# One slot and one tick: moving the side work of a three-block transformer kernel in TensorE's order

## The chip, the cores and the metric

The kernel runs on one core of a Trainium2 chip. The metric is device time in microseconds, the median of three runs. TensorE, VectorE, ScalarE, GpSimd and SyncE each work through their own list of instructions in order; semaphores tie the lists together.

## The reference, cut to what matters

256 tokens of width 2048 pass through three transformer blocks. Only the first one is touched:

```
h    = rms_norm(x)
p_r, p_k, p_v, z_r, q, k, v, z_a, m_r, m_a = split(h @ w_in)
y_r  = rwkv7(h, p_r, p_k, p_v) * silu(z_r)           # a recurrence over the tokens, 16 heads of 64
y_a  = chunk_band_attention(q, k, v) * silu(z_a)     # 16 heads of 64
x    = x + rms_norm((sigmoid(m_r) * (y_r @ w_r) + sigmoid(m_a) * (y_a @ w_a)) @ w_out)
```

The attention is softmax(q k + bias) v over a band of chunks. The recurrence is

```
S = S * w_t + (S @ -kk_t) (kk_t * a_t) + v_t k_t ;  y_t = S r_t
```

with kk normalised per head and y normalised per head afterwards (mean, variance, reciprocal root). The kernel computes it in chunks of 64 tokens.

## The kernel before

**Main work.** All large products are a stream of slots: 512 rows of a weight matrix by 256 columns, in fp32 made of a high and a low half. Per slot TensorE does 8 products of 512 columns (high half, L2516) and 8 of 256 columns (low half, L2520). ScalarE makes the high half of the weights (L2419), VectorE the low half (L2426), both two slots ahead ("the split of slot q+2"); SyncE loads the weights. Four slots make a block in the sections of this document. The sections stand at these slots: qkv from 0, za from 48, rkv from 64, gates from 112, zr from 176, branch from 192. At a block's end ScalarE copies a part of the sums out of PSUM (L2027), VectorE adds the rest (L2129), and the block is rescaled by the norm: by VectorE in rkv and zr (L2133), by GpSimd in gates (L2071). In rkv VectorE then mixes neighbouring tokens (L2139, L2142). These follow the split on VectorE.

**Side work.** The attention, the recurrence and other small work run as threads beside the stream. A thread is a set of generators, one per engine, that yield ticks. A tick t stands at start + t x pace, in slots, and class Beside runs it at the next of the three places of a slot on that engine: q, q+0.34 and q+0.67. On TensorE the place q stands ahead of the slot's products, q+0.34 after four wide ones, q+0.67 after eight (in rkv every second slot has the narrow products first). On VectorE the place q stands after L2129 of a block that just ended and ahead of the split of slot q+2 and of the rescaling; q+0.34 stands after both. On ScalarE q stands after L2027 and ahead of the split. So the ticks alone set each engine's order of instructions.

**Attention1** (two threads, for even and odd pairs of heads, always called one behind the other) has four rounds of 12 ticks at a pace of 0.85. Steps of a round: VectorE scales q (L767), ScalarE reverses k and v into place (L797, L798), TensorE turns v and makes the scores of the first head of the pair (L824 to L832), VectorE adds the bias and takes the maximum (L773 to L777), TensorE makes the second head's scores, which needs the first ones read ("scored0", L774), then exp on ScalarE (L805, L807), probabilities on VectorE (L781 to L784), their transposes (L842) and the products with v (L848 to L850) on TensorE, and the gate on VectorE (L789).

**Rwkv** (two threads, even and odd pairs of heads) starts one slot into gates, at slot 113, at a pace of 0.28. Its first norms are done ahead of the rounds: squares on VectorE (L953, L955), sums on TensorE (`norms`), a reciprocal root in Newton steps on VectorE (`roots`, L959, L90 to L95, L965), spread on TensorE (`norm_spread`), product (`normed`, L969). Then four rounds of 66 ticks begin at tick FIRST = 8: decay logits (TensorE), tanh (ScalarE), "sigmoid" (VectorE, L987), cumulated sums (TensorE), exponentials (ScalarE, L1072 to L1075), r_hat, z_hat, b_hat, k_hat (VectorE, L994 to L999), products ab and ak (TensorE), a triangular inverse in five doubling steps (y1/xx1 to y5/xx5; copies L1086 on ScalarE, sums L1016 and L1018 on VectorE), four chunk steps (w, sa, st for c = 0 to 3; L1090 on ScalarE, L1023, L1035, L1037 on VectorE), then mean, variance (L1045, L90 to L95), its spread and the normalised y (L1052 to L1057). All products of this class stand at L1105. The next round's norms are done within a round.

zr's blocks on VectorE (L2174) need y of the rounds; branch needs all of it.

Of the kernel before, what the change touches and what calls it, by code (L numbers as in the profile page):

```python
# [118 lines left out]
def build_kernel(nc, I, out_dram):  # L119
    ctx = ExitStack()  # L120
    with ctx:
# [171 lines left out]
        def par(name, c=0, n=1):  # L293
            return prm[:, rows[name] + c:rows[name] + c + n]
# [569 lines left out]
        class Rwkv:  # L864
# [11 lines left out]
                PE += [f"w{c}", f"sa{c}"] + ([f"st{c}"] if c < 3 else [])  # L876
            PE += ["o", "mean", "var", "var_spread"]
            TICKS = 66
            FIRST = 8

            def __init__(self, th, take, more):
                self.th = th
# [31 lines left out]
            def gpsimd(self, pool):  # L914
                dv, ac, pe_, po = self.dv, self.ac, self.pe_, self.po
                for i in range(4):
                    j, t0 = 2 * i + self.th, self.FIRST + self.TICKS * i
                    yield t0
# [24 lines left out]
            def vector(self, v):  # L943
# [5 lines left out]
                def squares(i):  # L949
                    k = k_[:, 2 * i + self.th, :]  # L950
                    if i:
                        dv.wait(v, "b_hat", i - 1)
                    self.dk.did(v.tensor_scalar(self.kn, k, par("k_k", 2 * i + self.th), None, ALU.mult), "kk")  # L953
                    self.dk.wait(v, "kk", i)
                    self.dk.did(v.tensor_tensor(self.sqr, self.kn, self.kn, ALU.mult), "kk_squared")  # L955

                def roots(i):
                    self.pk.wait(v, "kk_norm", i)
                    self.dk.did(v.tensor_scalar(self.nrm, x[:, 128:132], 1e-30, None, ALU.max), "norm_copied")  # L959
                    if self.th == 1:  # L960
                        for rw in rwkv:
                            rw.dk.wait(v, "norm_copied", i)
                        norm_roots.did(rwkv_root.run(v, *rwkv_eight), "rooted")
                        norm_roots.wait(v, "rooted", i)
                        norm_roots.did(v.tensor_scalar(rwkv_eight[1], rwkv_eight[1], 1e12, None, ALU.min), "inverted")  # L965

                def normed(i):
                    self.pk.wait(v, "norm_spread", i)
                    self.dk.did(v.tensor_tensor(self.kn, x[:, 256:512], self.kn, ALU.mult), "kk_normed")  # L969
                    self.dk.wait(v, "kk_normed", i)  # L970
                for i in range(4):
                    j, t0 = 2 * i + self.th, self.FIRST + self.TICKS * i
                    pr = lambda name: par(name, j)
                    if i == 0:
                        yield 0
                        v.wait_ge(mixed, 36)
                        v.wait_ge(masks_made, MASKS)
                        v.wait_ge(lora_activated, 9)
                        squares(0)
                        yield 2  # L980
                        roots(0)
                        yield 6
                        normed(0)
                    yield t0 + 2
                    ac.wait(v, "decay", i)
# [60 lines left out]
                    if self.th == 1:  # L1046
                        for rw in rwkv:
                            rw.dv.wait(v, "variance", i)
                        deviation_roots.did(rwkv_root.run(v, *rwkv_eight), "inverted")
                    yield t0 + 66  # L1050
                    pe_.wait(v, "var_spread", i)
                    dv.did(v.tensor_tensor(self.y, y[:, 0:256], self.y, ALU.mult), "y_normed")  # L1052
                    dv.wait(v, "y_normed", i)
# [6 lines left out]
            def scalar(self, act):  # L1060
# [3 lines left out]
                for i in range(4):  # L1064
                    t0 = self.FIRST + self.TICKS * i
                    yield t0 + 1
# [31 lines left out]
            def tensor(self, pe):  # L1098
# [13 lines left out]
                def norms(i):  # L1112
                    self.dk.wait(pe, "kk_squared", i)
                    for t in range(2):
                        m = mm(x[:, 128 + 2 * t:130 + 2 * t], self.sqr[:, t * P:(t + 1) * P], headpair)
                    self.pk.did(m, "kk_norm")

                def norm_spread(i):
                    norm_roots.wait(pe, "inverted", i)
                    self.pk.did(spread(x[:, 256:512]), "norm_spread")  # L1120
                for i in range(4):
                    j, t0 = 2 * i + self.th, self.FIRST + self.TICKS * i
                    if i == 0:
                        yield 1
                        norms(0)
                        yield 4
                        norm_spread(0)
                    yield t0
                    if i:
# [110 lines left out]
                    for t in range(2):  # L1240
                        m = mm(x[:, 256 + 2 * t:258 + 2 * t], self.ysq[:, t * P:(t + 1) * P], headpair)
                    pe_.did(m, "var")
                    yield t0 + 65
                    deviation_roots.wait(pe, "inverted", i)
                    pe_.did(spread(y), "var_spread")

# [959 lines left out]
        at = lambda name, b=0.0: S[name].slot0 + b * S[name].slots  # L2206
# [2 lines left out]
        threads.append(Thread("lora", 0, 0.5, sync=lora_sync, gpsimd=lora_pool, vector=lora_vector, tensor=lora_tensor, scalar=lora_scalar))  # L2209
        att1 = [Attention1(0, low, 7424, variance), Attention1(1, high, 14336, variance_t)]  # L2210
        for th in range(2):
            att1[th].thread(at("rkv", 0.25), 0.85)
        pieces = [[(high, 2048, 6656)], [(high, 6656, 8192), (low, 7424, 9472), (high, 14336, 16384)]]

        def taker(spans):
# [383 lines left out]
```

## Time and profile before

| | |
|---|---|
| median of 3 runs | 3461.02 us (3460.91 to 3462.06) |
| the profiled execution's own time | 3464.4 us |
| its span, first to last instruction | 3462.7 us |
| mean granted TensorE clock | 0.989 |
| TensorE busy | 3373.7 us, 97% |
| VectorE busy | 2204.5 us, 64% |
| ScalarE busy | 1540.7 us, 44% |
| GpSimd busy | 295.4 us, 9% |

Stages of the profile: the side work of Attention1 lies between about 225 and 335 us (rkv), that of Rwkv between 393 and 820 us (gates and zr). A row of a timeline gives start, duration, engine, line, operation, output and inputs; in brackets stands the idle time of the engine just before it and what ended it. A granted clock of 1.00 is TensorE's full speed (2.4 GHz), 0.50 the lower level (1.2 GHz).

### The profile page before, as it was taken

To read this page: it belongs to the slowest core of one execution; us is meant where nothing else is said; L and a number is where in the kernel's file an instruction comes from. 1 tells how busy PE (TensorE), PEld (TensorE's weight loads), DVE (VectorE), ACT (ScalarE), POOL (GpSimd) and SP (SyncE) were. 2 spreads that over 40 slices of the span, in tenths; PEclk is the share of its full clock that TensorE was granted. 3 is DMA by queue.
4 is the path that set the end of the run, shared out by engine and by line. 5 is a ranking of instruction groups with operands and counts; after the bars stand their busy time and mean duration, and the time that the engine had idled before them with its cause. 6 is when DMAs were issued, how large, how long until landed. Compare 5 with 4: busy or idle time off the path is not lost.

```text
span 3462.7 us, 52014 instructions
## 1 busy us (share of the span) xinstructions
PE 3373.7 (97%) x21718; PEld 2915.4 (84%) x21718; DVE 2204.5 (64%) x3044; ACT 1540.7 (44%) x2117; POOL 295.4 (9%) x318
## 2 busy tenths in 40 slices
PE   8999999999989999999999999999999999999998
PEld 7888877778878888888888888888888888888887
DVE  5567655556667576777666446655677866446654
ACT  4454433334553445544544444444354544334443
POOL 3100122220011101110100000001000100000000
PEclk9999999999999999999999999999999999999999
DMA  5554433335635555655555665565554556556554
GB/s 190 178 180 154 137 111 111 111 107 184 195 126 160 185 158 167 197 161 170 194 182 185 195 193 186 184 200 180 175 158 159 183 179 211 194 182 194 190 199 146
DMA packets 550751, 592.98 MB, mean 171 GB/s; under 512 B 16757, under 2 KB 511733, under 8 KB 550262
## 3 DMA queue, kind: packets, MB, share of 16 engines
q1 hardware_dynamic: 550518, 589.66, 52.6%
q8 instruction: 172, 2.82, 0.3%
q14 instruction: 61, 0.50, 0.0%
HBM read 583.24 MB, written 6.32 MB: 170 GB/s over the span
## 4 chain that ended last, share of the span: by engine, by line
PE 88%; DVE 7%; ACT 2%; issue 2%; DMA 1%; POOL 0%; SPq 0%; DVEq 0%; ACTq 0%; POOLq 0%
PE gp L2516 45%; PE gp L2520 24%; PE gp L2501 7%; PE sidep L1105 4%; PE gp L2506 3%; DVE w_parts L2426 2%; ACT w_parts L2419 1%; DMA high<-bias_rows 0%; DVE stage L2133 0%; ACT lo_half L2027 0%; PE sidep L560 0%; PE sidep L1345 0%; DVE stage L2129 0%; DVE low L2165 0%; PE sidep L1430 0%
## 5 line engine op out<-in xcount | busy, mean ns | idle before, releaser
L2426 DVE TENSOR_TENSOR w_parts<-ring,w_parts 128x1024 fp32r<-128x1024 f32 x1084 | 1365.8, 1282 | 456.1 <-ACT w_parts L2419 454.9
L2516 PE MATMUL gp<-x_parts,w_parts 128*128 128x512 f32 x5840 | 1482.9, 398 | 11.4 <-issue 5.5
L2419 ACT ACTIVATE w_parts<-ring 128x1024 fp32r<-128x1024 f32 x1084 | 1109.0, 1052 | 453.5 <-PE gp L2506 189.0
L2516 PEld LDWEIGHTS gp<-x_parts,w_parts 128*128 128x128 f32 x5840 | 1062.9, 190 | 215.9 <-issue 10.3
L2520 PEld LDWEIGHTS gp<-x_parts,w_parts 128*128 128x128 f32 x5840 | 773.3, 192 | 47.9 <-issue 5.9
L2520 PE MATMUL gp<-x_parts,w_parts 128*128 128x256 f32 x5840 | 802.3, 285 | 2.6 <-DVE w_parts L2426 2.6
L2027 ACT ACTIVATE lo_half<-gp 128x512 f32<-128x512 f32 x239 | 142.8, 597 | 896.5 <-PE gp L2516 460.9
L2516 PE MATMUL gp<-ff_parts,w_parts 128*128 128x512 f32 x1792 | 430.8, 391 | 0.0
L2516 PEld LDWEIGHTS gp<-ff_parts,w_parts 128*128 128x128 f32 x1792 | 328.6, 188 | 63.0
L2129 DVE TENSOR_TENSOR stage<-gp,lo_half 128x512 f32<-128x512 f32 x168 | 116.0, 690 | 378.7 <-ACT lo_half L2027 377.8
L2501 PE MATMUL gp<-w_parts,ff_parts 128*128 128x512 f32 x1024 | 273.7, 389 | 0.0
L2520 PEld LDWEIGHTS gp<-ff_parts,w_parts 128*128 128x128 f32 x1792 | 230.9, 191 | 10.6 <-issue 0.9
L2520 PE MATMUL gp<-ff_parts,w_parts 128*128 128x256 f32 x1792 | 235.4, 283 | 0.3 <-DVE w_parts L2426 0.3
L2501 PEld LDWEIGHTS gp<-w_parts,ff_parts 128*128 128x128 f32 x1024 | 192.3, 188 | 39.8
L528 POOL TENSOR_TENSOR low<-low 128x512 f32<-128x512 f32 (+1 forms) x38 | 58.9, 1557 | 1238.2 <-ACT low L519 648.9
L2506 PE MATMUL gp<-w_parts,ff_parts 128*128 128x512 f32 x512 | 157.7, 389 | 0.0
L2129 DVE TENSOR_TENSOR high<-gp,lo_half 128x512 f32<-128x512 f32 x63 | 43.5, 690 | 166.4 <-ACT lo_half L2027 166.3
L2043 ACT ACTIVATE ff_parts<-stage 128x512 fp32r<-128x512 f32 x64 | 40.5, 632 | 166.6 <-DVE stage L2167 166.6
L2506 PEld LDWEIGHTS gp<-w_parts,ff_parts 128*128 128x128 f32 x512 | 96.1, 188 | 20.0
L1105 PEld LDWEIGHTS sidep<-high 64*64 64x64 f32 x1696 | 62.6, 136 | 42.9 <-issue 18.6
L2071 POOL TENSOR_TENSOR high<-high,rstd 128x512 f32<-128x512 f32 x40 | 58.7, 1467 | 459.8 <-DVE high L2129 459.8
L1105 PE MATMUL sidep<-high 64*64 64x64 f32 (+1 forms) x1696 | 75.9, 237 | 16.2 <-DVE high L997 4.6
(391 smaller groups left out, 1868.6 us busy)
## 6 DMA issues: line engine op xcount, KB each, us to landing
ring<-w_in SPq DMA_DIRECT2D x220, 1024.0 KB, 5.1
ring<-w_ff SPq DMA_DIRECT2D x128, 1024.0 KB, 5.6
ring<-w_up SPq DMA_DIRECT2D x64, 1024.0 KB, 5.8
ring<-w_down SPq DMA_DIRECT2D x64, 1024.0 KB, 5.0
ring<-w_out SPq DMA_DIRECT2D x48, 1024.0 KB, 5.2
ring<-w_branch_attn SPq DMA_DIRECT2D x8, 1024.0 KB, 5.2
ring<-w_branch_rwkv SPq DMA_DIRECT2D x8, 1024.0 KB, 5.2
gate_scratch<-stage SPq DMA_DIRECT2D x16, 256.0 KB, 2.3
```

The source lines that it names most:

```text
L528: m = pool.tensor_tensor(self.acc[k], self.acc[k], self.sq[b - 1][k], ALU.add)
L1105: return pe.matmul(out, lhs, rhs, start=start, stop=stop, skip_group_check=True)
L2027: act.activation(lo_half[:, k % 2], gp[:, k % 2, :, 1, :], ACT.Copy).then_inc(lo_copied, 1)
L2043: act.activation(ff_parts[:, 2 * b:2 * b + 2, 0, :], st, ACT.Copy).then_inc(ff_high_split, 1)
L2071: pool.tensor_tensor(to, to, over(rstd, 2), ALU.mult).then_inc(scaled_by_pool, 1)
L2129: v.tensor_tensor(to, gp[:, k % 2, :, 0, :], lo_half[:, k % 2], ALU.add).then_inc(block_evacuated, 1)
L2419: act.activation(w_parts[:, q % PARTS, 0], ring[:, u % RING, SLOT * (q % 2):SLOT * (q % 2) + SLOT, :], ACT.Copy).then_inc(high_split, 1)
L2426: v.tensor_tensor(w_parts[:, q % PARTS, 1], ring[:, u % RING, SLOT * (q % 2):SLOT * (q % 2) + SLOT, :], w_parts[:, q % PARTS, 0].bitcast(F ...
L2501: pe.matmul(wide_sums(k, t), operand(s, b, s.chunks * n + c)[:, half, tokens], w[:, 0, c, :], start=(n == 0 and c == 0 and half == 0), sto ...
L2506: m = pe.matmul(wide_sums(k, t), operand(s, b, s.chunks * n + c)[:, 0, tokens], w[:, 1, c, :], start=False, stop=(n == s.slots - 1 and c = ...
L2516: return pe.matmul(gp[:, k % 2, j, :, :], w_parts[:, q % PARTS, 0, c, j * P:(j + 1) * P], operand(s, b, SLOT * n + c), start=(n == 0 and c ...
L2520: return pe.matmul(gp[:, k % 2, j, 0, :], w_parts[:, q % PARTS, 1, c, j * P:(j + 1) * P], operand(s, b, SLOT * n + c)[:, 0, :], start=Fals ...
```

## The change

Five numbers and two conditions in the ticks:

- FIRST goes from 8 to 9: all rounds of the recurrence a tick (0.28 slots) later, on all four engines.
- Its first norms: TensorE's sums go from tick 1 to 4, its spread from 4 to 7; VectorE's root from 2 to 4.8, the product from 6 to 8. The squares stay at tick 0.
- The last round's spread of the variance on TensorE goes from tick 65 of the round to 67, the normalised y on VectorE from 66 to 68; in the other rounds they stay.
- Attention1 starts at slot 66, not 65: all its steps one slot later, on all engines and SyncE.

Nothing is added or taken away.

```
-            FIRST = 8
+            FIRST = 9
...
                         squares(0)
-                        yield 2
+                        yield 4.8
                         roots(0)
-                        yield 6
+                        yield 8
                         normed(0)
...
-                    yield t0 + 66
+                    yield t0 + (66 if i < 3 else 68)
                     pe_.wait(v, "var_spread", i)
...
-                        yield 1
+                        yield 4
                         norms(0)
-                        yield 4
+                        yield 7
                         norm_spread(0)
...
-                    yield t0 + 65
+                    yield t0 + (65 if i < 3 else 67)
                     deviation_roots.wait(pe, "inverted", i)
...
-            att1[th].thread(at("rkv", 0.25), 0.85)
+            att1[th].thread(at("rkv", 0.5), 0.85)
```

**VectorE at the end of block 88 (in rkv), third round of Attention1.** L773 to L777 read the scores; L2129 begins what follows the block's end, L2142 ends it. Before:

```order
L773 TENSOR_TENSOR low<-sidep,low 128x128
L774 TENSOR_TENSOR low<-sidep,low 128x256
...
L2129 TENSOR_TENSOR stage<-gp,lo_half 128x2x256
L2426 TENSOR_TENSOR w_parts<-ring,w_parts 128x1024
L2133 TENSOR_TENSOR stage<-stage,rstd 128x2x256
L2139 TENSOR_TENSOR high<-stage 128x512
L2142 SCALAR_TENSOR_TENSOR high<-high,prm,stage 128x256 x2
```

The change:

```order
L2129 TENSOR_TENSOR stage<-gp,lo_half 128x2x256
L2426 TENSOR_TENSOR w_parts<-ring,w_parts 128x1024
L2133 TENSOR_TENSOR stage<-stage,rstd 128x2x256
L2139 TENSOR_TENSOR high<-stage 128x512
L2142 SCALAR_TENSOR_TENSOR high<-high,prm,stage 128x256 x2
L773 TENSOR_TENSOR low<-sidep,low 128x128
L774 TENSOR_TENSOR low<-sidep,low 128x256
```

The first scores of the round stood ahead of the block's end and now stand behind its mixing.

**TensorE from slot 87 on, the same round.** L824 to L832 with x2 of ident are v's transposes and the first scores; the L831 and L832 without them are the second scores. Before:

```order
L832 MATMUL sidep<-high 128x256
L2516 MATMUL gp<-x_parts,w_parts 128x512 x4
L2520 MATMUL gp<-x_parts,w_parts 128x256 x16
L2516 MATMUL gp<-x_parts,w_parts 128x512 x8
L831 MATMUL sidep<-low,high 128x128
```

The change:

```order
L832 MATMUL sidep<-high 128x256
L2516 MATMUL gp<-x_parts,w_parts 128x512 x12
L2520 MATMUL gp<-x_parts,w_parts 128x256 x8
L831 MATMUL sidep<-low,high 128x128
```

The second scores stood at the end of block 88 and now stand one slot behind it, at slot 89.

**TensorE at slots 113 to 115, the first norms of Rwkv.** headones,high is the sum of squares, ident,smalls the spread of the root, sidep<-low the decay logits. Before:

```order
L2516 MATMUL gp<-x_parts,w_parts 128x512 x4
L1105 MATMUL sidep<-headones,high 128x2 x4
L2516 MATMUL gp<-x_parts,w_parts 128x512 x4
L2520 MATMUL gp<-x_parts,w_parts 128x256 x8
L2516 MATMUL gp<-x_parts,w_parts 128x512 x4
L1105 MATMUL sidep<-ident,smalls 64x128 x8
L2516 MATMUL gp<-x_parts,w_parts 128x512 x4
L2520 MATMUL gp<-x_parts,w_parts 128x256 x8
L2516 MATMUL gp<-x_parts,w_parts 128x512 x4
L1105 MATMUL sidep<-low 128x128 x4
```

The change:

```order
L2516 MATMUL gp<-x_parts,w_parts 128x512 x8
L2520 MATMUL gp<-x_parts,w_parts 128x256 x8
L2516 MATMUL gp<-x_parts,w_parts 128x512 x4
L1105 MATMUL sidep<-headones,high 128x2 x4
L2516 MATMUL gp<-x_parts,w_parts 128x512 x4
L2520 MATMUL gp<-x_parts,w_parts 128x256 x8
L1105 MATMUL sidep<-ident,smalls 64x128 x8
L2516 MATMUL gp<-x_parts,w_parts 128x512 x8
L1105 MATMUL sidep<-low 128x128 x4
```

The sums of squares come a slot later, the spread two thirds of a slot, the decay logits a third.

**ScalarE at the end of block 172 (in gates), head of the fourth round of Rwkv.** L1068 is tanh for "sigmoid", L2027 the block's copy, L2419 a pass of high halves, L1072 to L1075 the exponentials of one pair of heads. Before:

```order
L1068 ACTIVATE low<-sidep 128x256
L2419 ACTIVATE w_parts<-ring 128x1024
L2027 ACTIVATE lo_half<-gp 128x512
L1072 ACTIVATE high<-sidep,consts 128x256
...
L1075 ACTIVATE smalls<-sidep 128x4
L2419 ACTIVATE w_parts<-ring 128x1024 x2
```

The change:

```order
L1068 ACTIVATE low<-sidep 128x256
L2027 ACTIVATE lo_half<-gp 128x512
L2419 ACTIVATE w_parts<-ring 128x1024
L1072 ACTIVATE high<-sidep,consts 128x256
...
L1075 ACTIVATE smalls<-sidep 128x4
L2419 ACTIVATE w_parts<-ring 128x1024
```

The exponentials stood ahead of both passes behind the block's end and now stand between them; tanh moved the other way, behind the pass ahead of the block's end.

At the end of the last round the variance on TensorE comes a third of a slot later and its spread a whole slot (190, not 189); VectorE's order is the same there.

## Rows read from the trace of the kernel before

**Rows 1.** The page, part 1: busy time, share of the span, instructions.

```profile
PE 3373.7 (97%) x21718; PEld 2915.4 (84%) x21718; DVE 2204.5 (64%) x3044; ACT 1540.7 (44%) x2117; POOL 295.4 (9%) x318
```

**Rows 2.** The page, part 4: the chain that ended last, by engine.

```profile
PE 88%; DVE 7%; ACT 2%; issue 2%; DMA 1%; POOL 0%; SPq 0%; DVEq 0%; ACTq 0%; POOLq 0%
```

**Rows 3.** TensorE's waits, 340 to 840 us: total us, times, longest us.

```profile
PE sidep L1105 <- DVE high L987: 5.5, 4, 1.6
PE sidep L1105 <- DVE high L997: 4.6, 2, 3.4
...
PE sidep L1105 <- DVE high L955: 3.4, 2, 2.5
PE sidep L1105 <- DVE smalls L95: 2.4, 1, 2.4
...
PE gp L2520 <- DVE w_parts L2426: 0.4, 1, 0.4
```

**Rows 4.** TensorE's waits, 25 to 340 us, the one in Attention1.

```profile
PE sidep L842 <- DVE low L784: 1.3, 2, 1.1
```

**Rows 5.** Windows, TensorE: length, busy (instructions), granted clock, DMA share, GB/s.

```profile
401.20:404.60 3.40, 3.40 (x14) 0.51 0.43 132
725.50:729.00 3.50, 3.50 (x40) 0.51 0.14 45
814.30:817.70 3.40, 3.08 (x19) 0.50 0.08 12
```

**Rows 6.** Timeline, TensorE, ab and ak of the fourth round.

```profile
724.55 5.38 PE L1105 MATMUL sidep<-high 64*64 64x128 f32 x64 [3.42 <-DVE high L997]
```

**Rows 7.** Timeline, TensorE, the last round's spread of the variance.

```profile
814.62 1.97 PE L1105 MATMUL sidep<-ident,smalls 128*64 128x128 f32 x16 [2.36 <-DVE smalls L95]
```

**Rows 8.** Timeline, TensorE, two slots without side work.

```profile
378.13 2.08 PE L2520 MATMUL gp<-x_parts,w_parts 128*128 128x256 f32 x16
...
383.69 2.08 PE L2520 MATMUL gp<-x_parts,w_parts 128*128 128x256 f32 x16
```

**Rows 9.** Timeline, VectorE, behind the end of block 88.

```profile
310.59 0.69 DVE L2129 TENSOR_TENSOR stage<-gp,lo_half 128x512 f32<-128x512 f32 x1 [1.85 <-ACT lo_half L2027]
311.54 1.23 DVE L2426 TENSOR_TENSOR w_parts<-ring,w_parts 128x1024 fp32r<-128x1024 f32 x1 [0.25 <-ACT w_parts L2419]
...
314.13 0.88 DVE L2142 SCALAR_TENSOR_TENSOR high<-high,prm,stage 128x256 f32<-128x256 f32 x2
314.93 0.28 DVE L773 TENSOR_TENSOR low<-sidep,low 128x128 f32<-128x128 f32 x1
...
316.10 0.28 DVE L773 TENSOR_TENSOR high<-sidep,high 128x128 f32<-128x128 f32 x1
```

**Rows 10.** Timeline, TensorE, first row behind the end of block 88.

```profile
309.86 0.49 PE L831 MATMUL sidep<-low,high 64*128 64x128 f32 x2
```

**Rows 11.** Timeline, ScalarE, k and v of one pair staged.

```profile
301.72 0.42 ACT L797 ACTIVATE low<-high 128x256 f32<-128x256 f32 x1 [4.59 <-DVE high L767]
302.04 0.40 ACT L798 ACTIVATE low<-high 128x256 f32<-128x256 f32 x1
```

**Rows 12.** Timeline, TensorE, the first norms' sums of squares.

```profile
399.40 0.61 PE L1105 MATMUL sidep<-headones,high 128*128 128x2 f32 x4 [2.53 <-DVE high L955]
400.84 0.38 PE L1105 MATMUL sidep<-headones,high 128*128 128x2 f32 x2 [0.82 <-DVE high L955]
```

**Rows 13.** Timeline, VectorE, first and last of the first root's 13 instructions.

```profile
401.84 0.22 DVE L959 TENSOR_SCALAR smalls<-sidep 128x4 f32<-128x4 f32 x2
...
405.76 0.17 DVE L965 TENSOR_SCALAR smalls<-smalls 128x8 f32<-128x8 f32 x1
```

**Rows 14.** Timeline, VectorE, ahead of ab in the fourth round.

```profile
722.26 1.23 DVE L2426 TENSOR_TENSOR w_parts<-ring,w_parts 128x1024 fp32r<-128x1024 f32 x1 [0.80 <-ACT w_parts L2419]
...
724.07 0.42 DVE L997 TENSOR_TENSOR high<-high 128x256 f32<-128x256 f32 x1
```

**Rows 15.** Timeline, VectorE, a pass of low halves in gates beside GpSimd's rescaling.

```profile
414.54 2.29 DVE L2426 TENSOR_TENSOR w_parts<-ring,w_parts 128x1024 fp32r<-128x1024 f32 x1
```

## The prediction

> **What bounds the kernel now.** I read the engine totals first, then the chain that ended last, then TensorE's waits stage by stage, then the rows around single waits. TensorE is busy for 97% of the span and holds 88% of the chain [rows 1, 2]. So a change of order gains or loses only where TensorE stands still, or where its granted clock falls. In the stage of the recurrence (340 to 840 us) the waits sum to 29.1 us in 21 pieces of 13 groups; among the larger groups are those for "sigmoid" (L987), b_hat (L997), the first norms' squares (L955) and the inverse root (L95), and the smallest is 0.4 us [rows 3]. In the stage of the first attention (25 to 340 us) there is hardly one: 1.3 us [rows 4]. The reader should keep in mind that the change moves a stage where almost nothing was lost, and one where 29 us were.
>
> **The clock of a wait.** Each of the half-clock stretches lies at or just behind a wait. From 725.5 to 729.0 the granted clock was 0.51, and from 814.3 to 817.7 it was 0.50: the 1.2 GHz level, after TensorE had waited 3.42 us and 2.36 us [rows 5 to 7]. Some 3.4 us at half rate cost 1.7 us each. The recurrence has six such stretches, the first at 401.2 and the last at 814.3 [rows 5]; the stage of the first attention has none.
>
> **The unit of the sum.** A slot is eight products of 512 columns and eight of 256; two slots take 5.56 us (378.13 to 383.69) [rows 8], so a slot is 2.78 us, with 0.91 us for four wide products and 0.96 us for eight narrow ones. VectorE and ScalarE run about a slot ahead of TensorE, except at a block's end (every fourth slot). There they wait for TensorE. I count from T, the moment the block's last product is done. At T = 309.86 the copy out of PSUM ran from T+0.73 to T+1.42, the low halves of the slot after next to T+2.9, and the scaling and mixing of r, k, v ended at T+5.15; only then came what stands a third of a slot later (314.93) [rows 9, 10]. A TensorE step behind such a chain waits for it.
>
> **First attention a slot later.** The four rounds' steps now meet block ends at other points. Third round: VectorE's first scores stand behind the mixing, which begin at T+5.1 and take 1.17 us a head, half of it for the scores that TensorE wants [rows 9]: T+5.7 for the first head of the pair and T+6.9 for the second; TensorE asks one slot after T, at T+2.8. It waits 2.9 + 0.4 = 3.3 us. Before, both stood a slot earlier and nothing waited. Fourth round: the second scores (2.4 us for both heads) come between the copy and the low halves, the mixing ends at T+7.3, and the probabilities (0.8 us a head) at T+8.1; TensorE asks at T+5.6: 2.5 + 0.2 = 2.7 us. Second round: q is scaled behind the mixing, and ScalarE's staging of a head takes 0.7 us from there (301.72 to 302.44) [rows 11], so that it ends at T+6.2 with 0.3 for the scaling; TensorE asks at T+4.65: 1.5 us. Its probabilities end at T+5.95, asked for at T+4.65: 1.5 us with the second head. First round: 0.7 for scores and 0.8 for probabilities, less the 1.1 that were there: +0.4. Sum 9.4 us. The two longest (2.9 and 2.5) are longer than the 2.36 that had the clock fall: 2 x 1.7 = 3.4. Together **+12.8 us**. Bounds: +5 (VectorE a microsecond or so earlier everywhere, no clock loss) to +17 (every wait over 1.4 us lowers the clock). The table's DMA and GpSimd's masks move by the same slot on their queues, and have the same slot and a third as before ahead of the scores: nothing.
>
> **First norms later.** TensorE waited 2.53 + 0.82 us for the squares [rows 12]. Asked for a slot later, the first head's are done and the second's cost 0.8 (they end at 400.8). But the root chain (4.1 us, 401.84 to 405.93 [rows 13]) now stands behind one more pass of low halves: two passes of 1.2 follow the squares, to 403.1, and the chain ends at 407.1. TensorE, which does one slot and the norms' 1.1 us between (399.5 to 403.3), comes for the spread at 403.3 and waits 3.8. That is 4.6 against 3.35: **+1.2**. The half clock stays where it was, a little later. Bounds: -1.7 to +2.5.
>
> **The rounds a tick later.** Each step moves by one place (a third of a slot), some by none. What decides is which side of a block's end a step lands on. Gains: fourth round's head. There ScalarE's exponentials stood directly behind the block's end and ahead of the high halves, so VectorE's low halves ended at 723.5 and b_hat at 724.5; TensorE waited 3.42 [rows 6, 14]. Now the exponentials follow the high halves, the chain is done at about T+5.8, TensorE asks at T+5.9, and of the sigmoid wait (1.6) 0.5 is left: -5.2 with what the order of the spread adds. The other gains: slot 128 -0.6, slot 135 -1.0, slot 161 -1.15, slot 164 -0.4, slot 180 -0.6. In all -8.95. Losses: in the first round "sigmoid" falls from ahead of the low halves to behind them, and r_hat too, +3.1 by slot 118; and steps that VectorE did ahead of a block's end now follow the copy (T+1.4) while TensorE asks within 0.9 us: slot 140 +1.2, slot 148 +1.0, slot 168 +0.8, slot 176 +2.15; ScalarE's copy at slot 120 +1.7; slot 132 +0.75, slot 144 +0.2, slots 153 to 156 +1.75. In all +12.65. Net **+3.7**, with as many half-clock stretches going (three) as coming. Bounds: -9 (no loss, all gains) to +10 (the reverse, about).
>
> In these blocks GpSimd rescales the block just copied. That instruction lay beside VectorE's pass of low halves, which took 2.29 us instead of the 1.23 us of the row at 311.54 [rows 9, 15]. The steps now behind that pass inherit the microsecond; I counted it eight times, 4.2 us in all. The Trainium skill ("SBUF — State Buffer", section "SBUF: two separate sides") says why: a VectorE instruction with two inputs in SBUF and a GpSimd one that reads SBUF share a port pair as an exclusive lock, and whichever starts first blocks the other. The trace agrees (+1.06 us). Were the rule not to hold in the new order, the total would be 4.2 us lower.
>
> **The last round's variance.** TensorE waited 2.36 us for the root [rows 7]. VectorE's order there is unchanged, TensorE asks a slot later, and does the variance itself a third later; ScalarE's squares now delay the high halves by 0.75, so the chain ends at T+6.9 where TensorE comes at T+6.7. The wait shrinks to 0.45: -1.9, and -1.7 for the clock: **-3.6**. What is next late is y_normed, which ends some 4 us ahead of the last zr block that needs it: nothing. Bounds -4.1 to 0.
>
> **Sum.** 12.8 + 1.2 + 3.7 - 3.6 = +14.1 us. The profiled run took 3464.4 us (span 3462.7), so its successor would take 3478.5. The runs' median is 3461.0, 3.4 less: 3475.1 us, 0.41% more.
>
> **Rivals.** (1) Faster, one mechanism: a wait moves work instead of adding it. While TensorE stands, the other two engines get ahead, and the chains behind the following block ends start from a better state, so that the rounds' new waits at the block ends (12.65) vanish and half of the attention's remains. 14.1 - 12.65 - 6.4 - 3.4 (two half-clock stretches more gone) = -8.35: 3453. It decides if TensorE finds VectorE's step done at slots 118, 120, 140, 148 and 176. Against it: chains there start at the block's end, whatever happened before. For it: the fourth round's head, where a third of a slot is worth 5 us. (2) No change: attention's waits come out at the lower bound (+5) since VectorE's scores need less than I count, and the rounds at -3.5: 14.1 - 7.8 - 7.2 = -0.9, or 3460, up to 3467. For it: 29 us of waits are redrawn, and what I place by hand within 0.3 us can fall either way. (3) The change does not do what it says: excluded, the orders show each step moved.
>
> **How the numbers follow.** This measurement can tell about 0.2% (6.9 us) from no change. My forecast, slower by 7 to 24 us, has 0.62; rival 2 has 0.22; rival 1 has 0.16. The range: from 3455, which takes in rival 2 and leaves out most of rival 1, to 3483, which is attention at its upper bound (+4.2) and half of the way to the rounds' (+3.2). The forecast's own range is 3468 to 3483. Faster 0.16, same 0.22, slower 0.62.
>
> **What would show it.** TensorE's waits between 180 and 340 us: some 10 us, one of 2.9 on L774, one of 2.5 on L784, one of 1.5 on ScalarE's L798. At the first norms: the wait on L955 under 1 us, one of nearly 4 on L95. The b_hat wait of 3.4 us at the fourth round gone, and one of about 2 us on L1016 at slot 176. The last L95 wait under 0.6. Span between the first norms and the end of zr: about the same as before. If the attention's stage shows under 3 us of waits, the forecast is wrong.

## The result and the profile after

The changed kernel takes 3481.3 us (median of 4 runs, 3477.5 to 3482.9), the kernel before 3461.0 beside it: 1.0056 times as long, interval 1.0044 to 1.0068. That is 20.3 us more, where +14.1 was forecast; 3475.1 was predicted, in a range of 3455 to 3483. The profiled execution took 3482.85 us, span 3481.1.

The page of the kernel after, part 1, busy time [rows 1], and part 4, the chain [rows 2]:

```profile
PE 3379.9 (97%) x21718; PEld 2919.6 (84%) x21718; DVE 2208.6 (63%) x3044; ACT 1542.3 (44%) x2117; POOL 294.0 (8%) x318
...
PE 86%; DVE 8%; ACT 2%; issue 2%; DMA 1%; SPq 0%; POOL 0%; DVEq 0%; ACTq 0%; POOLq 0%
```

TensorE's waits after, 25 to 345 us, the larger rows (total us, times, longest us; before: [rows 4]):

```profile
PE sidep L831 <- DVE low L774: 2.9, 1, 2.9
PE sidep L824 <- ACT low L798: 1.4, 1, 1.4
PE sidep L842 <- DVE low L784: 1.1, 1, 1.1
```

The same view, 340 to 860 us (before: [rows 3]; the last round of the attention now ends behind 340):

```profile
PE sidep L1105 <- DVE high L987: 7.2, 4, 3.3
PE sidep L1105 <- DVE smalls L965: 3.9, 1, 3.9
PE sidep L1105 <- DVE high L1023: 3.7, 3, 1.6
PE sidep L1105 <- DVE high L1016: 3.7, 3, 2.1
PE sidep L1105 <- DVE high L997: 2.7, 2, 2.6
PE sidep L842 <- DVE low L784: 2.2, 1, 2.2
...
PE gp L2520 <- DVE w_parts L2426: 1.3, 1, 1.3
```

The b_hat wait of 3.42 and the last root's of 2.36 [rows 6, 7] have no row any more. New are the waits of the attention, that for the first root (L965, 3.9) and one of 2.1 on L1016. Windows of TensorE after (length, busy and instructions, granted clock, DMA share, GB/s), at five of the stretches at the 1.2 GHz level (before: [rows 5]):

```profile
272.00:278.80 6.80, 6.80 (x17) 0.50 0.47 155
323.20:326.60 3.40, 3.40 (x13) 0.50 0.28 81
374.40:377.80 3.40, 3.29 (x10) 0.50 0.25 75
422.20:429.00 6.80, 6.04 (x27) 0.50 0.47 155
435.80:439.20 3.40, 3.40 (x14) 0.51 0.00 0
```

The first three lie in the attention's stage, which had none before.

**Accounts of all kernels.** The stream is the same in every kernel, so I cut each trace where TensorE starts slots 64, 113 and 192, add up TensorE's waits (all that the profile names, from 0.15 us on), and add up the time at the low clock (1.2 GHz), of which half is lost. One execution of each kernel has a trace, so the waits and the low clock are those of one execution; the median and the ratio are of all. Each label stands again at its experiment below. The kernel before, run beside each group, had medians of 3460.5 to 3461.7 us.

| kernel | 64 to 113: us / waits / low clock | 113 to 192: us / waits / low clock | median, ratio to before [interval] |
|---|---|---|---|
| before | 175.3 / 1.3 / 0 | 429.8 / 28.5 / 20.5 | 3461.0 |
| after | 190.8 / 9.1 / 13.7 | 432.2 / 30.4 / 20.5 | 3481.3, 1.0056 [1.0044, 1.0068] |
| att_slot_alone | 188.5 / 8.8 / 10.2 | 424.6 / 28.5 / 10.2 | 3471.4, 1.0031 [1.0018, 1.0044] |
| recurrence_alone | 175.4 / 1.3 / 0 | 431.9 / 30.9 / 20.5 | 3466.4, 1.0016 [1.0007, 1.0024] |
| first_norms_alone | 175.4 / 1.3 / 0 | 432.3 / 30.0 / 23.9 | 3462.3, 1.0004 [0.9994, 1.0013] |
| last_spread_alone | 175.4 / 1.3 / 0 | 425.7 / 26.7 / 17.1 | 3458.8, 0.9993 [0.9984, 1.0002] |
| rounds_tick_alone | 175.4 / 1.3 / 0 | 430.9 / 31.8 / 13.7 | 3466.3, 1.0014 [1.0006, 1.0023] |
| scores_before_mixing | 182.5 / 5.9 / 3.4 | 431.8 / 30.4 / 20.5 | 3474.0, 1.0037 [1.0024, 1.0051] |
| head4_and_last | 175.4 / 1.3 / 0 | 419.7 / 22.8 / 10.2 | 3453.2, 0.9976 [0.9965, 0.9986] |
| picked_ticks | 175.4 / 1.3 / 0 | 412.9 / 19.6 / 3.4 | 3447.4, 0.9956 [0.9943, 0.9968] |
| att_block_later | 176.1 / 1.8 / 0 | 428.8 / 28.5 / 20.5 | 3463.3, 1.0003 [0.9994, 1.0013] |
| rescale_thin | 193.7 / 9.1 / 20.5 | 422.4 / 25.8 / 10.2 | 3473.7, 1.0033 [1.0021, 1.0046] |
| asked_later | 175.4 / 1.3 / 0 | 410.8 / 15.8 / 10.2 | 3442.6, 0.9946 [0.9934, 0.9959] |
| busy_root | 193.8 / 9.1 / 20.5 | 429.7 / 27.5 / 10.2 | 3482.0, 1.0056 [1.0041, 1.0070] |

Length less waits less half the low clock is the same everywhere: 174.0 to 174.9 us in the first stage, and 389.9 to 392.3 in the second (busy_root less its added products). So a change of these ticks costs or gives its waits and its low clock, and nothing else to within some 2 us. Behind slot 192, where nothing was changed, the traces still take 2632.1 to 2638.7 us, with 38.5 to 50.9 us of low clock: that much of a difference of times is not the change's.

### The profile page after: what moved, and what is told of

Same layout as the page of the kernel before. It is cut to its first block, busy times and chain, and to the rows that moved or that the text cites. A ratio compares the mean times of both kernels' runs of the same rounds, so it can differ in the third digit from the quotient of the medians.

```text
span 3481.1 us, 52012 instructions
## 1 busy us (share of the span) xinstructions
PE 3379.9 (97%) x21718; PEld 2919.6 (84%) x21718; DVE 2208.6 (63%) x3044; ACT 1542.3 (44%) x2117; POOL 294.0 (8%) x318
## 4 chain that ended last, share of the span: by engine, by line
PE 86%; DVE 8%; ACT 2%; issue 2%; DMA 1%; SPq 0%; POOL 0%; DVEq 0%; ACTq 0%; POOLq 0%
PE gp L2516 44%; PE gp L2520 24%; PE gp L2501 7%; PE sidep L1105 4%; PE gp L2506 3%; DVE w_parts L2426 2%; ACT w_parts L2419 1%; DVE stage L2133 0%; DMA high<-bias_rows 0%; PE sidep L560 0%; ACT lo_half L2027 0%; DVE stage L2129 0%; DMA ring<-w_branch_rwkv 0%; PE sidep L1345 0%; SPq L2250 0%
## 5 line engine op out<-in xcount | busy, mean ns | idle before, releaser
L2419 ACT ACTIVATE w_parts<-ring 128x1024 fp32r<-128x1024 f32 x1084 | 1110.2, 1053 | 443.6 <-PE gp L2506 188.9
L2027 ACT ACTIVATE lo_half<-gp 128x512 f32<-128x512 f32 x239 | 142.9, 598 | 909.6 <-PE gp L2516 473.9
L2129 DVE TENSOR_TENSOR stage<-gp,lo_half 128x512 f32<-128x512 f32 x168 | 116.2, 691 | 379.4 <-ACT lo_half L2027 378.4
L2129 DVE TENSOR_TENSOR high<-gp,lo_half 128x512 f32<-128x512 f32 x63 | 43.5, 691 | 164.6 <-ACT lo_half L2027 164.5
L1105 PEld LDWEIGHTS sidep<-high 64*64 64x64 f32 x1696 | 62.0, 135 | 42.8 <-issue 23.2
L1105 PE MATMUL sidep<-high 64*64 64x64 f32 (+1 forms) x1696 | 75.2, 235 | 15.7 <-DVE high L1023 3.7
```

The costliest lines, as they stand in the source:

```text
L1105: return pe.matmul(out, lhs, rhs, start=start, stop=stop, skip_group_check=True)
L2027: act.activation(lo_half[:, k % 2], gp[:, k % 2, :, 1, :], ACT.Copy).then_inc(lo_copied, 1)
L2129: v.tensor_tensor(to, gp[:, k % 2, :, 0, :], lo_half[:, k % 2], ALU.add).then_inc(block_evacuated, 1)
L2419: act.activation(w_parts[:, q % PARTS, 0], ring[:, u % RING, SLOT * (q % 2):SLOT * (q % 2) + SLOT, :], ACT.Copy).then_inc(high_split, 1)
```

## The experiments

### Each part alone

**The attention alone** (att_slot_alone).

```
-            att1[th].thread(at("rkv", 0.25), 0.85)
+            att1[th].thread(at("rkv", 0.5), 0.85)
```

> The kernel before with the first attention alone started a slot later; the recurrence is as before. Theory (the parts add up): the traces of the two kernels stand 15.5 us apart at slot 113, where the recurrence begins, so this kernel is 15.5 us slower than before (12 to 18), with waits of 1.44, 1.15, 2.90 and 2.23 us on L798, L784, L774 and L784 between 270 and 375 us and half-clock stretches of 6.8 + 3.4 + 3.4 us; its recurrence has the 29 us of waits of before. Rival (a delayed TensorE lets VectorE and ScalarE get ahead, so that the recurrence repays a part): +7 to +11, with the delay against before shrinking between slots 113 and 192. The sum on record priced this part at 12.8.

Measured: +9.7 us in the median (6 to 15 by the interval). The waits are those foretold, but the profiled execution lost 13.2 us up to slot 113 and got 5.2 back by slot 192. Behind slot 192, where the two kernels are the same, it got another 5.0 back. Its recurrence has the waits of before, 28.5 us, with half the low clock: 10.2 us, not 20.5. TensorE in this kernel at the b_hat wait of the fourth round:

```profile
735.62 3.71 PE L1105 MATMUL sidep<-high 64*64 64x128 f32 x64 [3.42 <-DVE high L997]
```

Its window behind that wait:

```profile
735.60:739.00 3.40, 3.38 (x62) 1.00 0.20 77
```

The same wait of 3.42 before had a clock of 0.51 behind it, and the 64 products took 5.38 us [rows 5, 6]; here the clock is 1.00 and they take 3.71. The median lies in the rival's range and not in the theory's. The rival's "repays" is there in size, but not as fewer waits: the low clock fell out otherwise.

**The rest alone** (recurrence_alone; the diff of the change without its last line).

> The changed kernel with the first attention back at its old slot. Theory (parts add up): the rest of the change, 18.4 - 15.5 = 3 us slower than before (1 to 5); no wait between 25 and 340 us longer than 1.1 us; the waits of the recurrence as in the changed kernel (3.9 on L965, 3.3 on L987, 2.1 on L1016). The sum on record: 1.2 + 3.7 - 3.6 = +1.3. Rival (the attention's delay had changed what the recurrence meets): the rest is no slower than before, 0 to -5 us.

+4.7 us (interval 2.4 to 8.3). Waits of parts add: 7.6 for the attention and 2.4 here make 10.0, and the full change has 9.7 more than before (the b_hat wait at slot 118 is 0.65 here and 0.15 there). The rival falls.

**The first norms alone** (first_norms_alone; the ticks 2, 6 and 1, 4 of the change).

> The kernel before with the ticks of the recurrence's first norms alone later (TensorE's sums 1 to 4, its spread 4 to 7, VectorE's root 2 to 4.8, product 6 to 8); the rounds stay. Theory: the wait for the squares falls from 3.35 to 0.8 us, one of 3.9 for the root takes its place, and the low clock behind it lasts 6.8 us instead of 3.4 (at the lower level that is 1.7 more): +3.0 us over before (1 to 4). Rival (the sum on record, no more low clock than before): +1.2. Second rival: the spread is now right ahead of the decay logits of the first round, which then wait for the product (tick 8 is also where the round begins): +4 or more.

```profile
407.45 1.92 PE L1105 MATMUL sidep<-ident,smalls 128*64 128x128 f32 x16 [3.92 <-DVE smalls L965]
```

That is TensorE's spread in this kernel. 0.83 + 3.92 us of waits stand where 2.53 + 0.82 stood [rows 12]: +1.4, the theory's waits. The low clock behind it was 3.4 us, not the 6.8 of the kernel after, so the low clock's 1.7 us is not seen, and the median (+0.6, interval -2 to +4.5) does not tell the three apart. The second rival's wait is not there: TensorE did not wait for the product ahead of the decay logits.

**The last spread alone** (last_spread_alone; the two lines with 67 and 68).

> The kernel before with the last round's spread of the variance alone later (TensorE's tick 65 to 67, VectorE's 66 to 68); the variance's sums stay where they were. Theory: the root is done 2.36 us after TensorE asked for it in the kernel before, and a slot of products is 2.78 us, two ticks 1.56: the wait falls to 0.5 or less and the half clock behind it goes: -1.9 - 1.7 = -3.6 us (-4 to -2). Rival (a wait of a later step takes its place, the normalised y or zr's gate): -1 to +1.

TensorE in this kernel, the spread, and the first wait behind it:

```profile
813.88 1.09 PE L1105 MATMUL sidep<-ident,smalls 128*64 128x128 f32 x16 [0.52 <-DVE smalls L95]
...
831.01 1.19 PE L2520 MATMUL gp<-x_parts,w_parts 128*128 128x256 f32 x8 [0.95 <-DVE w_parts L2426]
```

2.36 became 0.52 (-1.84), and no stretch of low clock lies behind it. The wait on the low halves behind the end of zr grew from 0.4 [rows 3] to 0.95: the normalised y now stands later on VectorE, ahead of these passes. The median is 3.0 us lower, but the interval takes in no change.

**The rounds' tick alone** (rounds_tick_alone; FIRST = 9).

> The kernel before with the recurrence's rounds alone a tick later (FIRST 9); first norms, attention and the last spread as before. Theory: losses in the first two rounds and the gain at the head of the fourth; from the two traces the delay grew by 2.4 us between slots 112 and 192 in the changed kernel, of which about +3 belong to the first norms and -3.6 to the last spread, so the rounds are worth about +3 (0 to +6). The sum on record: +3.7. Rival: the rounds alone are a gain of 2 to 5 us, and the changed kernel's loss there came from the delayed state in which the attention left the engines.

+4.6 us (2 to 8). TensorE in this kernel, three of its new or longer waits (slots 136, 153, 176):

```profile
528.43 3.71 PE L1105 MATMUL sidep<-high 64*64 64x128 f32 x64 [2.56 <-DVE high L997]
...
627.17 1.13 PE L1105 MATMUL sidep<-consts,high 128*128 128x256 f32 x4 [3.27 <-DVE high L987]
...
752.48 0.68 PE L1105 MATMUL sidep<-high 64*64 64x64 f32 x16 [2.10 <-DVE high L1016]
```

The waits grow by 3.3 us, as the theory has it, and the loss stands without any attention ahead of it: the rival falls.

### The attention's place

**One step moved back ahead of the mixing** (scores_before_mixing).

```
-                        yield t0 + 2 + 2 * hh
+                        yield t0 + (1.7 if i == 2 and hh == 0 else 2 + 2 * hh)
                         pe_.wait(v, f"s{hh}", i)
```

> The changed kernel, but VectorE takes the first scores of the attention's third round (L773, L774 of the first pair) one place earlier: directly behind the copy of the block that just ended, ahead of the low halves and the mixing. Theory (TensorE's 2.9 us stop is VectorE's order behind the block's end, and the low clock is the stop's): the wait of 2.90 us on L774 at slot 89 falls to 0.3 us or less and the half-clock stretch behind it goes: 2.6 + 1.7 = 4.3 us faster than the changed kernel (3 to 5), so 14 us over before. Rival (the wait moves): the low halves and the mixing are 0.6 us later, and TensorE waits for them or for the second scores instead: 0 to 2 us faster.

VectorE of the kernel after, from the low halves behind the end of block 88 to the first read of scores, and TensorE, which waited for it:

```profile
317.40 1.23 DVE L2426 TENSOR_TENSOR w_parts<-ring,w_parts 128x1024 fp32r<-128x1024 f32 x1 [0.25 <-ACT w_parts L2419]
...
320.99 0.41 DVE L774 TENSOR_TENSOR low<-sidep,low 128x256 f32<-128x256 f32 x1
...
321.46 0.48 PE L831 MATMUL sidep<-low,high 64*128 64x128 f32 x2 [2.90 <-DVE low L774]
```

With the step moved, VectorE and TensorE:

```profile
314.02 0.41 DVE L774 TENSOR_TENSOR low<-sidep,low 128x256 f32<-128x256 f32 x1
...
315.25 0.48 PE L831 MATMUL sidep<-low,high 64*128 64x128 f32 x2
```

The wait is gone, and the low halves and the mixing, now behind the scores, are late for nobody. The median is 7.3 us below the changed kernel's, which ran in another group, and 12.3 above before (8 to 18, where the changed kernel has 15 to 24); the stage's waits fell by 3.2, as expected, and its low clock by 10.2 (5.1 us), where one stretch (1.7 us) was expected.

**A whole block later** (att_block_later). at("rkv", 0.25) becomes at("rkv", 1.25).

> The kernel before with the first attention alone started four slots (one block) later than before, at slot 69; the recurrence is as before. Theory (what costs is where a step stands against a block's end, not that it is later): every step meets the block's ends as before, so TensorE's waits from slot 64 to 113 are the 1.3 us of before (0.5 to 3) and no stretch of low clock lies there; the time is that of before within 5 us. Rival (later is worse in itself, the fourth round runs up against the end of rkv and the norms of the recurrence): waits of 5 us or more, +6 to +12 us.

TensorE's waits in this kernel, 220 to 396 us:

```profile
PE sidep L842 <- DVE low L784: 1.3, 2, 1.1
PE sidep L824 <- ACT low L798: 0.5, 1, 0.5
```

Four slots later cost nothing that can be measured (+2.8, interval -2 to +4.5), with 1.8 us of waits; one slot later cost 7.6 us of waits. The rival falls. What costs is not "later" but where a step meets a block's end.

### The recurrence's ticks, picked

**Only what gains** (head4_and_last, then picked_ticks). The ticks go through a function; at first:

```
+            def later(self, i, t):
+                return 1 if i == 3 and t <= 10 else 0
...
+                            yield tick + self.later(i, t)
```

> The kernel before with two things: the last round's spread later (ticks 67 and 68), and in the fourth round alone the first ten ticks (decay logits to b_hat, ab and ak) one tick later on all engines. First attention, first norms and the other rounds stay. Theory: -3.6 for the spread, -5.2 (3.4 of wait, 1.7 of clock) for the head: 8.8 us faster than before (7 to 10), 0.25%. Rival (the head's gain in the changed kernel depends on the rounds before it being late too): -3 to -5.

TensorE of this kernel at "sigmoid" and at b_hat of the fourth round (line numbers shifted: L990 is L987, L1000 is L997, L1108 is L1105):

```profile
716.49 1.13 PE L1108 MATMUL sidep<-consts,high 128*128 128x256 f32 x4 [0.19 <-DVE high L990]
...
722.72 1.53 PE L1108 MATMUL sidep<-high 64*64 64x128 f32 x24 [0.51 <-DVE high L1000]
```

8.5 us below before (5 to 12): the theory. TensorE waits 0.51 us for b_hat where it waited 3.42, and 0.19 for "sigmoid" (1.63). So the head's gain needs no other round to be late.

```
+                return 1 if (i == 3 and t <= 10) or (i == 2 and 26 <= t <= 44) or (i == 0 and 44 <= t <= 50) else 0
```

> As the kernel before this one (the last spread, and the fourth round's first ten ticks a tick later), and the ticks 26 to 44 of the third round and 44 to 50 of the first a tick later too, where steps stood so that the tick saved a wait in the sum on record. Theory: 8.8 + 1.0 + 1.15 + 0.4, some 11 us faster than before (10 to 14). Rival: the steps now a tick closer to those behind them cost what they save: 7 to 10 faster.

14.3 us below before (11 to 20). Waits fell by another 3.2 us (2.5 expected), and the low clock to 3.4 us.

**TensorE alone later** (asked_later).

```
+                            if program == self.tensor:
+                                if tick == 1:
+                                    tick = 3
+                                if (i, t) in ((0, 61), (1, 3), (1, 8), (1, 38), (1, 40), (2, 3), (2, 14), (3, 50), (3, 52)):
+                                    tick += 1.2
```

> The kernel with the picked ticks (last spread, fourth round's head, parts of the third and first round a tick later), and now TensorE alone is later at ten steps at which it waited for 1.1 us or more in that kernel's trace: the first norms' sums by two ticks (wait 2.53), and by one place the sums of the first round's variance (1.26), cumulated sums and ab of the second round (1.63, 1.12), st0 and w1 of the second (1.58), cumulated sums and y1 of the third (1.57, 1.17), st2 and w3 of the fourth (1.96). Theory (a step that TensorE waits for comes at the same moment whether TensorE stands still or does four wide or eight narrow products of the stream, 0.91 to 0.96 us, meanwhile): -1.87 for the norms and -0.93 for each of seven others, -8.4 us against the picked ticks, and 22 to 24 us below before. Rival (each step moved comes too late for the next one on VectorE or ScalarE, and the waits come back one step on): under 3 us gained.

TensorE at "sigmoid" of the third round with the picked ticks (line numbers of this and the next are shifted by a few: L990 is L987, L1108 is L1105):

```profile
611.96 1.09 PE L2525 MATMUL gp<-x_parts,w_parts 128*128 128x512 f32 x4
614.63 1.13 PE L1108 MATMUL sidep<-consts,high 128*128 128x256 f32 x4 [1.57 <-DVE high L990]
```

and asked later:

```profile
609.78 2.00 PE L2530 MATMUL gp<-x_parts,w_parts 128*128 128x512 f32 x8
612.47 1.13 PE L1108 MATMUL sidep<-consts,high 128*128 128x256 f32 x4 [0.68 <-DVE high L990]
```

Four more wide products stand ahead, and 0.89 us of waiting is gone. Of the seven, six came out so (1.26 to 0.36, 1.63 to 0.69, 1.58 to 0.64, 1.57 to 0.68, 1.17 to 0.26, 1.96 to 1.03: -5.5 us). The seventh, ab of the second round, still waits 1.13: its shift only made up for that of the cumulated sums ahead, which I had counted again. And the norms lost more than they gained:

```profile
399.44 0.61 PE L1108 MATMUL sidep<-headones,high 128*128 128x2 f32 x4 [0.68 <-DVE high L958]
...
406.00 1.98 PE L1108 MATMUL sidep<-ident,smalls 128*64 128x128 f32 x16 [2.97 <-DVE smalls L968]
```

The wait for the squares fell by 1.85, but those products are missing between sums and spread, where the root's chain is as long as before: 2.97 us, together +1.1. A wait of the fourth round's inverse (slot 174) grew from 0.50 to 1.08. Waits fell by 3.8 in all, less than half of the 8.4 of the theory. The median stands 4.8 us below that of the picked ticks, but the two ran in different groups and their intervals against before overlap, so the waits show this gain and the times do not. It is 17.9 us below before, where 22 to 24 was expected: 3442.6 us, 0.5%, the lowest median here.

### The port and the clock

**GpSimd's rescaling made thin** (rescale_thin).

```
+                if s.name == "gates":
+                    pool.tensor_tensor(to[:, :, 0:16], to[:, :, 0:16], over(rstd, 2)[:, :, 0:16], ALU.mult).then_inc(scaled_by_pool, 1)
```

> The changed kernel, but GpSimd's rescaling in the blocks of gates (L2071) works on 16 of the 256 columns of each half: most of the rescaling of gates is left out. Theory of the record (VectorE's pass of low halves takes 2.2 us beside it, not 1.23, and the side steps behind that pass inherit the microsecond, eight times 1 us, 4.2 us in all between slots 113 and 176): the passes at the block's ends fall to 1.3 us, TensorE's waits from slot 113 to 192 fall from 30.5 to some 26 us, and the kernel is 4 us faster than the changed one (2 to 7 with the clock). Rival (VectorE has enough slack behind most of these passes): the passes get shorter all the same, and the waits fall by under 2 us.

VectorE and GpSimd after, at the head of the second round:

```profile
542.31 1.50 DVE L995 SCALAR_TENSOR_TENSOR high<-high 128x256 f32<-128x256 f32 x1
...
542.14 1.38 POOL L2071 TENSOR_TENSOR stage<-stage,rstd 128x512 f32<-128x512 f32 x1 [1.92 <-DVE stage L2129]
```

With the rescaling thin:

```profile
542.98 0.48 DVE L995 SCALAR_TENSOR_TENSOR high<-high 128x256 f32<-128x256 f32 x1
...
542.81 0.36 POOL L2072 TENSOR_TENSOR stage<-stage,rstd 128x32 f32<-128x32 f32 x1 [1.93 <-DVE stage L2132]
```

VectorE's instruction took 1.02 us less, and TensorE's wait for b_hat behind it fell from 2.56 to 1.54. Of the 64 passes of low halves between slots 113 and 176, eight took over 2.1 us in the kernel after, as that of [rows 15] did before; here none does, and the longest takes 1.75. The waits fell from 30.4 to 25.8: 4.6 us, for 4.2 on record, so about half of what the passes lost reached TensorE. The median is 7.6 us below the changed kernel's, more than the 2 to 7 expected; what goes beyond the waits is not shown to be the rescaling's, since in the trace the low clock fell by 10.2 us in the recurrence and rose by 6.8 in the attention's stage, which was not touched. The Trainium skill ("SBUF — State Buffer", section "SBUF: two separate sides") has this as an exclusive lock held for the whole instruction; the rows agree, since L995 ends at 543.81, just behind GpSimd's 543.52.

**TensorE kept busy at the root** (busy_root).

```
+                    if i == 0 and self.th == 0:
+                        for n in range(12):
+                            mm(y[:, 0:256], headones[:, :], self.sqr)
                     norm_roots.wait(pe, "inverted", i)
```

> The changed kernel with 12 products of 256 columns that nobody reads (0.28 us each at full clock, 3.4 us) put on TensorE ahead of the spread of the first norms, where it waited 3.93 us for the root. Theory (the low clock follows from TensorE standing still): the wait falls to 0.5 us, the time of the spread is the same, and the 6.8 us at half clock that began at 422.2 in the changed kernel are gone or halved: 1.7 to 3.4 us faster. Rival (the low clock is not due to this wait): the stretch stays, and the time is that of the changed kernel, 0 to +1.

TensorE in this kernel, the added products, and its next wait:

```profile
421.82 5.34 PE L1105 MATMUL sidep<-high,headones 128*128 128x256 f32 x24
...
436.24 1.13 PE L1105 MATMUL sidep<-consts,high 128*128 128x256 f32 x4 [2.32 <-DVE high L987]
```

The window from 416 to 440 us in it and, as the second row, in the kernel after:

```profile
416.00:440.00 24.00, 20.84 (x127) 1.00 0.27 88
```

```profile
416.00:440.00 24.00, 17.30 (x84) 0.79 0.27 88
```

The clock stayed at 1.00 through the whole place. I had mis-sized the products: each is two passes of 0.22 us, so they took 5.3 us, and the spread began 1.2 us later behind slot 114 than in the kernel after; from slot 114 to 118 the kernel gained 2.3 us all the same. The wait of 2.32 behind is the old one (2.33 after), and the low stretch that began there at 435.8 is gone too. The whole kernel's median is that of the changed kernel, 3482.0 against 3481.3, so the time shows no gain. In the five traces with the wait of 3.9 us a low stretch of 3.4 or 6.8 us stood at it; in this one none did. That is one trace, and the stretches vary from trace to trace, so it speaks for the theory without settling it.

## Why the prediction was right, and where it was off

Slower was right, and most of the mechanism: the waits came where the prediction had them. The size came out low (14.1 for 20.3 us), and of the terms the clock of the attention's waits was the one most off. Of the 4.4 us by which the profiled execution (3482.85) missed the forecast for it (3478.5), the first stage has 2.7 (waits 1.6 less than forecast, low clock 3.4 more, 0.9 in neither), the recurrence 1.2 and the rest of the program 0.5. The median has another 1.8, since the profiled execution of before stood 3.4 us above its median and that of after only 1.6.

- **Attention, waits** (9.4): measured 7.8 (7.6 alone). The named ones came: 2.9 + 0.3 for the third round's scores (3.3), 2.2 for the fourth's probabilities (2.7), 1.4 for the second's q (1.5), 1.15 for its probabilities (1.5). The first round gained 0.8 where I had +0.4; one of 0.85 (L798, fourth round) was not foreseen.
- **Attention, clock** (3.4): the step that failed. The trace has 13.7 us of low clock, 6.8 us lost. I had taken the 2.36 us wait of the trace of before for the shortest that lowers the clock; here 6.8 us of it followed a wait of 1.44. The trace of before could have told: one of its six stretches stands at a wait of 0.80 us (timeline and window of the kernel before):

```profile
676.32 0.33 PE L1105 MATMUL sidep<-high 64*64 64x64 f32 x4 [0.80 <-ACT high L1090]
```

```profile
677.70:681.10 3.40, 3.40 (x11) 0.50 0.20 77
```

  Alone, the attention had no stretch at that same wait of 1.44, and 6.8 us at the 2.90. The length of a wait does not decide its low clock by itself. The four traces with all of these waits (after, att_slot_alone, rescale_thin, busy_root) lost 6.8, 5.1, 10.2 and 10.2 us to it in this stage: my 3.4 lay below all of them.
- **First norms** (+1.2): the waits came as worked out, 4.75 against 4.6, +1.4. The low stretch there was 6.8 us after, 3.4 before: 1.7 us that I had at nothing.
- **Rounds** (+3.7): +3.3 of waits with the tick alone, or +4.0 without the 0.7 that the last root gained by it. By place: up to slot 118 +2.7 (3.1), 120 +1.3 (1.7), 140 +1.2 (1.2), 153 to 156 +2.0 (1.75), 176 +2.1 (2.15), 161 -1.3 (-1.15), 164 -0.8 (-0.4), head of the fourth round -4.2 (-5.2). Not foreseen: b_hat of the second round (1.1 to 2.6), ScalarE's copy at slot 184 (+1.6), and against them 2.8 us gained on L1023 at 181 and 185, where I had 0.6.
- **Last variance** (-3.6): the wait as foretold, -1.84 for -1.9. "Next late: nothing" was wrong: the low halves behind zr wait for the later y (after: 1.3 and 0.7 us, before 0.4).
- **Port** (4.2): 4.6 measured. Eight passes a microsecond longer make 8 us on VectorE; the 4.2, which the prediction does not split up, fits what reached TensorE.
- **Rivals.** The first, that a wait moves work, is refuted: waits keep their size, to about 0.1 us, whatever stands ahead (28.5 us of them in the recurrence with and without 13 us of delay). The exception is b_hat at slot 118: 1.12 us in the three traces with this order and no low clock between slots 116 and 118 (rounds_tick_alone, rescale_thin, busy_root), and 0.15 to 0.65 in the three with a stretch there, where TensorE came later. The rival's -8 us would have needed slots 118, 120, 140, 148 and 176 free; TensorE waited for 1.0 to 2.1 us at four of them, and for 0.15 at 118. The second had the attention at +5 and no clock; it was 7.8 of waits alone.
- **Slips in the sums** that change nothing: 24 us over before would be 3485, not the 3483 at which the forecast's own range ends; all losses of the rounds without a gain are +12.65, not +10; and T+6.9 less T+6.7 is 0.2 for the last root, not 0.45.

## What to carry to other kernels

Where one engine is the stream and others serve it in blocks, a side step's price is its place against the block's end: a slot later cost 7.6 us of waits, a whole block later nothing. Move single steps, and where the stream waits for a step, let only the stream's engine ask later, by no more work than it waits; that work is then missing at the next wait, so look at the two together. Sum waits and low clock apart: waits repeat to a tenth of a microsecond and can be worked out ahead, the low clock cannot, and it needs several runs.

## What the runs showed of the hardware

- The low clock's cost of the same wait varies. Behind the b_hat wait of 3.42 us lay 3.4 us at 0.51 before, nothing in att_slot_alone, and a stretch of 6.8 in first_norms_alone, last_spread_alone and att_block_later. A wait of 0.80 had 3.4 us behind it before. Executions of the kernel before ran from 3454.6 us at a mean granted clock of 0.992 to 3467.5 at 0.988: as wide as most of the changes here. What decides it for one wait is open.
- VectorE's two-input instruction of 128x256 is held up by GpSimd's as the large passes are: 0.48 us beside the thin rescaling, 1.50 beside the whole.
- Low clock ahead of a wait takes part of the wait away, since TensorE asks later: at slot 118 it was 1.12 us without such a stretch and 0.15 to 0.65 with one.
